# The gates' 16 columns ride behind the first head's values as moving columns

## The reference

```python
(sb, scg, sx, mq, mk, mv, mo, mg, dq, dk, dv, gs, gm, gd) = split_cols(u @ w_in + b_in)
...
g = mg.astype(jnp.float32).reshape(b, t, 4, ML_HEADS).transpose(2, 0, 3, 1)
gates = (g[0], g[1], jax.nn.log_sigmoid(g[2]), jax.nn.log_sigmoid(g[3]))
```

## Time and profile before

| | us |
|---|---|
| median of 3 runs | 2347.71 |
| lowest, highest | 2346.6, 2347.77 |
| span of the profiled execution | 2345.9 |
| TensorE busy in it | 2324.3 (99%) |
| VectorE busy | 1658.6 (71%) |
| ScalarE busy | 1034.5 (44%) |
| the 24 products of the gates, each layer | 5.44 |

### The profile page before, as it was taken

How to read it: one execution, slowest core, us unless ns; L and a number is a source line. 1 busy time by engine, 2 the same in 40 slices (tenths; PEclk the granted TensorE clock), 3 DMA queues, 4 the chain that set the end, 5 groups by cost and what they waited for, 6 DMA issues and landing times.

```text
span 2345.9 us, 35713 instructions
## 1 busy us (share of the span) xinstructions
PE 2324.3 (99%) x12926; PEld 2024.5 (86%) x12926; DVE 1658.6 (71%) x2777; ACT 1034.5 (44%) x1765; POOL 194.4 (8%) x186
## 2 busy tenths in 40 slices
PE   8999999999999999999999999999999999999998
PEld 6888889888888888898888898888898898999997
DVE  6998577457757655669885368886665757878876
ACT  5423224435556544363222264322245347756554
POOL 2111000000000000021120000111100000001220
PEclk9999999999999999999999999999999999999999
DMA  8788465232222322338783328776544433656654
GB/s 276 241 249 246 127 213 149 82 95 76 73 68 81 95 81 70 110 91 254 237 246 113 94 80 249 232 237 181 180 117 117 117 99 103 172 143 196 193 160 141
DMA packets 540057, 356.89 MB, mean 152 GB/s; under 512 B 15206, under 2 KB 490896, under 8 KB 539920
## 3 DMA queue, kind: packets, MB, share of 16 engines
q1 hardware_dynamic: 538472, 354.70, 51.6%
q10 hardware_dynamic: 1448, 0.38, 0.1%
HBM read 337.20 MB, written 17.83 MB: 151 GB/s over the span
## 4 chain that ended last, share of the span: by engine, by line
PE 94%; DVE 2%; ACT 1%; issue 1%; DMA 1%; POOL 0%; DVEq 0%; SPq 0%; ACTq 0%; POOLq 0%
PE ps L1101 25%; PE ps L1103 25%; PE ps L1102 25%; PE ps L1401 2%; PE ps L1402 2%; PE ps L1400 2%; PE ps L1114 1%; PE ps L1475 1%; PE ps L1193 1%; PE ps L1195 1%; PE ps L1194 1%; PE ps L1512 1%; PE ps L1116 1%; DVE w_lo L2350 0%; PE ps L1413 0%
## 5 line engine op out<-in xcount | busy, mean ns | idle before, releaser
L1618 ACT ACTIVATE w_hi<-raw 128x1024 fp32r<-128x1024 f32 (+3 forms) x430 | 423.3, 985 | 848.9 <-PE ps L1103 661.1
L2350 DVE TENSOR_TENSOR w_lo<-raw,w_hi 128x1024 fp32r<-128x1024 f32 (+3 forms) x430 | 495.0, 1152 | 423.1 <-ACT w_hi L1618 417.6
L1101 PE MATMUL ps<-u_hi,w_hi 128*128 128x512 f32 (+2 forms) x2176 | 778.1, 358 | 1.1 <-DVE w_lo L2350 0.7
L1103 PE MATMUL ps<-u_hi,w_lo 128*128 128x512 f32 (+2 forms) x2176 | 773.5, 355 | 0.0
L1102 PE MATMUL ps<-u_lo,w_hi 128*128 128x512 f32 (+2 forms) x2176 | 773.1, 355 | 0.0
L1101 PEld LDWEIGHTS ps<-u_hi,w_hi 128*128 128x128 f32 x2176 | 411.2, 189 | 60.1 <-issue 1.3
L1103 PEld LDWEIGHTS ps<-u_hi,w_lo 128*128 128x128 f32 x2176 | 411.1, 189 | 57.7
L1102 PEld LDWEIGHTS ps<-u_lo,w_hi 128*128 128x128 f32 x2176 | 411.4, 189 | 55.8
L2768 DVE SCALAR_TENSOR_TENSOR ada_acc<-ada_in_up,cs,ada_acc 128x512 f32<-128x512 f32 x378 | 284.2, 813 | 0.0
L1101 PE MATMUL ps<-g,w_hi 128*128 128x512 f32 (+1 forms) x572 | 206.9, 362 | 0.0
L1102 PE MATMUL ps<-g,w_hi 128*128 128x512 f32 (+1 forms) x572 | 204.1, 357 | 0.0
(11 more groups left out here) (394 smaller groups left out, 3678.0 us busy)
## 6 DMA issues: line engine op xcount, KB each, us to landing
raw<-in_ffn_up SPq DMA_DIRECT2D x150, 512.0 KB, 4.8
raw<-in_w_in SPq DMA_DIRECT2D x132, 512.0 KB, 3.8
ada_in_up<-in_w_ada SPq DMA_DIRECT2D x108, 512.0 KB, 4.6
raw<-in_ffn_down SPq DMA_DIRECT2D x67, 384.0 KB, 3.6
fold_out<-ada_acc SPq DMA_DIRECT2D x32, 512.0 KB, 3.5
fold<-fold_out SPq DMA_DIRECT2D x32, 512.0 KB, 5.4
raw<-in_ffn_down SPq DMA_DIRECT2D x42, 320.0 KB, 3.2
h<-in_ffn_up SPq DMA_DIRECT2D x22, 512.0 KB, 4.0
```

The source lines that it names most:

```text
L1101: pe.matmul(ps[bank][:, cols_of], wh, a_hi, start=a, stop=False)
L1103: m = pe.matmul(ps[bank][:, cols_of], wl, a_hi, start=False, stop=b)
L1618: act.activation(hi, whole, ACT.Copy).then_inc(hi_done, 1)
L2350: dve.tensor_tensor(lo, whole, hi.bitcast(F32), ALU.subtract).then_inc(lo_done, 1)
```

## The change

The gates' columns become moving columns. The first group of values is cut in two: chunks mv0 to mv3 hold head 0's 256 columns and behind them the gates' 16 (272 in all), mv4 to mv7 head 1's 256, mv8 to mv11 the last two heads' 512. Each of the first four has a second transfer for the 16 columns. The first values group now comes before mk0 to mk3, so the order is cg1, mv0 to mv3, mk0 to mk3, mv4 to mv11, sx1, sb1. On emptying the first group VectorE also copies the 16 columns of each token tile into a cleared tile `gate_rows`, spread in four groups, and TensorE turns that tile in four transposes behind mk0. The 24 products, the early transfer and `gate_weights` go. The gate steps stand behind mk0, mk3, mv5 and mv8.

```diff
-CH_UP, CH_DOWN, CH_PROJ, CH_WO = 2 * KF, 4 * KD, 48, KD
+CH_UP, CH_DOWN, CH_PROJ, CH_WO = 2 * KF, 4 * KD, 52, KD
...
-GATES_BEHIND = (0, 4, 5, 8)
+GATES_BEHIND = (4, 7, 9, 12)
...
-    for n in range(12):
-        order.append(("mk", n) if n < 4 else ("mv", n - 4))
-        if n in (6, 8):
-            order.append(("qk_high" if n == 6 else "qk_low", 0))
+    for n in range(16):
+        order.append(("mk", n - 4) if 4 <= n < 8 else ("mv", n if n < 4 else n - 4))
+        if n in (10, 12):
+            order.append(("qk_high" if n == 10 else "qk_low", 0))
...
+VALUE_TILES = (("mv", 0, 2), ("mv", 2, 2), ("mv", 4, 4), ("dv", 0, 4))
+GATE_COLS = 16
+VALUE_WIDTH = [n * P + (GATE_COLS if group == 0 else 0) for group, (_, _, n) in enumerate(VALUE_TILES)]
...
-                sp.dma_start(wg_in[:, :, :], w_in[layer, :, MG_COL:MG_COL + 16].rearrange("(k p) n -> p k n", p=P)
-                             ).then_inc(wg_landed, 16)
...
+                    sp.dma_start(dst[:, :, 0:n * P], src[:, k:k + 2, col:col + n * P]).then_inc(raw_in[slot], 16)
+                    if group == 0:
+                        sp.dma_start(dst[:, :, n * P:n * P + GATE_COLS], src[:, k:k + 2, MG_COL:MG_COL + GATE_COLS]
+                                     ).then_inc(gates_landed[step[1] % RAW], 16)
...
-                    pe.matmul(ps[t][:, :], u_hi[:, k, own], wh, start=(k == 0), stop=False)
-                    pe.matmul(ps[t][:, :], u_lo[:, k, own], wh, start=False, stop=False)
-                    m = pe.matmul(ps[t][:, :], u_hi[:, k, own], wl, start=False, stop=(k == KD - 1))
+                    pe.matmul(ps[t][:, 0:width], u_hi[:, k, own], wh, start=(k == 0), stop=False)
+                    pe.matmul(ps[t][:, 0:width], u_lo[:, k, own], wh, start=False, stop=False)
+                    m = pe.matmul(ps[t][:, 0:width], u_hi[:, k, own], wl, start=False, stop=(k == KD - 1))
...
-            pe.wait_ge(wg_ready, layer + 1)
-            for k in range(KD):
-                pe.wait_ge(u_ready, u_count(3 * layer + 1, 1, k))
-                for n, (w, a) in enumerate(((wg_hi, u_hi), (wg_hi, u_lo), (wg_lo, u_hi))):
-                    m = pe.matmul(ps[6][:, :], w[:, k, :], a[:, k, :], start=(n == 0 and k == 0),
-                                  stop=(n == 2 and k == KD - 1))
+            pe.wait_ge(evac_dve, BASES[layer, "proj"][2] + PLANS[layer]["mv", 3][3] + 1)
+            for t in range(TT):
+                m = pe.transpose(ps[6][:, t * P:(t + 1) * P], gate_rows[:, t, :], ident)
...
-            for w in (wg_hi, wg_lo):
-                pool.memset(w[:, :, :].bitcast(F32), 0.0).then_inc(wg_cleared, 1)
+            pool.memset(gate_rows[:, :, :], 0.0).then_inc(rows_cleared, 1)
...
-                if f == 0:
-                    gate_weights(layer)
...
+                if group == 0:
+                    m = dve.tensor_copy(gate_rows[:, t, :].rearrange("p (q n) -> p q n", q=4)[:, :, 0:HEADS],
+                                        ps[t][:, tiles * P:tiles * P + GATE_COLS].rearrange("p (q n) -> p q n", q=4))
+                m.then_inc(evac_dve, 1)
```

More of the change, by code:

```diff
@@ L325, with value_width @@
 BESIDE_ML = range(FIRST_ML - 3, FIRST_ML + 5 * HEADS)
-assert [NTH_PROJ[n] for n in (FIRST_ML - 5, FIRST_ML - 4)] == [("mv", 6), ("mv", 7)] and FIRST_ML % 4 == 3
+assert [NTH_PROJ[n] for n in (FIRST_ML - 5, FIRST_ML - 4)] == [("mv", 10), ("mv", 11)] and FIRST_ML % 4 == 3
 FIRST_AFTER = (0, 1, 3, 5)
-X_FIRST = ORDERS[0][4:ORDERS[0].index(("mk", 0))]
+X_FIRST = ORDERS[0][4:ORDERS[0].index(("mv", 0))]
 PROJ_BANK = [n % (2 if n in BESIDE_ML else 4) for n in range(CH_PROJ)]
 assert all(n % 4 == v[1] % 4 for n, v in NTH_PROJ.items() if v[0] in VALUES)
+assert all(PLANS[layer][step][0] == n for layer in range(DEPTH) for n, step in NTH_PROJ.items())
+def value_width(c):
+    step = NTH_PROJ.get(c)
+    if step is None or step[0] not in VALUES or VALUE_WIDTH[VALUES[step[0]] + step[1] // 4] == BLOCK:
+        return None
+    return VALUE_WIDTH[VALUES[step[0]] + step[1] // 4]
 SCORE_ML = (6, 7, 2, 3)
@@ L560, in apart_rows, with split_views @@
         return slice(3 * q - 3, 3 * q - 3 + len(LAST_K[q]) // 2), seg_order(n)[1][1]
-    def split_views(r, slot, raw_slot, kn):
+    def split_views(r, slot, raw_slot, kn, width=None):
         raw_view = raw_tiles(raw_slot, kn)
+        if width is not None:
+            return [a.rearrange("p (k n) -> p k n", k=2)[:, :, 0:width]
+                    for a in (w_hi[:, slot, :], w_lo[:, slot, :], raw[:, raw_slot, :])]
         if not is_apart(r):
@@ L1387, in values @@
             base, part = BASES[layer, "proj"][0], i % 4
-            slot = (base + r) % SPLIT
+            slot, width = (base + r) % SPLIT, VALUE_WIDTH[VALUES[kind] + i // 4]
             pe.wait_ge(lo_done, base + r + 1)
@@ L1610, in silu_table, with split @@
             act.activation(small[:, 15:16], small[:, 0:1], ACT.Silu)
-        def split(r, slot, place, kn=KD):
+        def split(r, slot, place, kn=KD, width=None):
             wait(act, chunk_used, split_room(r))
@@ L1616, in split, with ahead @@
             act.wait_ge(raw_in[raw_slot], landed)
-            hi, _, whole = split_views(r, slot, raw_slot, kn)
+            hi, _, whole = split_views(r, slot, raw_slot, kn, width)
             act.activation(hi, whole, ACT.Copy).then_inc(hi_done, 1)
-        def ahead(base, c, i=0, step=0, kn=KD):
+        def ahead(base, c, i=0, step=0, kn=KD, width=None):
             r = base + c + SPLIT
@@ L1624, in ahead @@
                 return
-            split(r + step * i, r % SPLIT, raw_place(base, c + SPLIT, i, step), kn)
+            split(r + step * i, r % SPLIT, raw_place(base, c + SPLIT, i, step), kn, width)
         for a, tile, r0, n in VECTOR_ROWS[0::2]:
@@ L1884, in proj @@
             t0 = t0_of(layer, kind in X_ONLY)
-            ahead(base, r)
+            later = NTH_PROJ.get(r + SPLIT, (None, 0))
+            if later[0] == "mv" and later[1] < 4:
+                act.wait_ge(gates_landed[later[1] % RAW], 16 * (2 * layer + later[1] // RAW + 1))
+            ahead(base, r, width=value_width(r + SPLIT))
             if kind in ("sx", "mk", "mv", "dv"):
@@ L2343, in after, with split, ahead @@
             dve.wait_ge(dve_chain, value)
-        def split(r, slot, place, kn=KD):
+        def split(r, slot, place, kn=KD, width=None):
             dve.wait_ge(hi_done, r + 1)
             wait(dve, chunk_used, split_room(r))
-            hi, lo, whole = split_views(r, slot, place[0], kn)
+            hi, lo, whole = split_views(r, slot, place[0], kn, width)
             dve.tensor_tensor(lo, whole, hi.bitcast(F32), ALU.subtract).then_inc(lo_done, 1)
-        def ahead(base, c, i=0, step=0, kn=KD):
+        def ahead(base, c, i=0, step=0, kn=KD, width=None):
             r = base + c + SPLIT
```

58 lines of the change are left out of this document (27 added, 31 removed).

## The result

The changed kernel takes 2363.57 us (median; 2362.27 to 2364.29) against 2347.0 us for the kernel before, run beside it: ratio 1.0069, 95% interval [1.0058, 1.0081]. It is 16.6 us slower. The forecast was 2358.5 us in a range that ended at 2363, 10.8 us above the 2347.7 that it started from; the direction held, the size was 5 to 6 us short. The difference of 0.69% lies well above the 0.2% that can be told here.

What follows compares the result with a forecast made beforehand. TensorE, busy for 99% of the span, was taken to bound the kernel. From 2347.7 us, layer 0 at +2.6 and layer 1 at +6.3 gave 2356.6; one clock fall, +2, made the forecast 2358.5 us, range 2355.5 to 2362.

Steps and rivals of the forecast that it cites:

- The arithmetic: TensorE's products and transposes, if nothing waits: -3.02 us per layer, -6.0 in all.
- The waits ahead of mv8: TensorE waits for VectorE to empty mv4's bank behind gate steps and splits: 5.4 us in layer 0, 4.5 in layer 1.
- mv0 in layer 1: First values chunk of layer 1 needs all four banks within 3 us and waits for their emptying: cost 3.6 us.
- mk0: mk0 waits for mv0's bank, emptied behind mk2's split: 0.1 us in layer 0, 1.1 in layer 1.
- What was costed at nothing: Extra loads, gate-column transfers, smaller splits, removed instructions and the gates' last step: covered, with no wait of their own.
- The clock: TensorE's clock falls behind one of the two long waits, about 2 us: +2, bounds 0 and 4.
- two falls: Rival: the clock falls behind both long waits, 2360.5 us; 75% together with the forecast and the no-fall case.
- worse: Rival: the gate columns' tiny rows hold up loads by over 1 us each, more short chunks starve: 2363 and up, 7%.
- One place alone: Rival: only layer 1's early queue costs, 2346.4 us, or only the waits before mv8, 2351.6 or 2353.6; 12%.
- the faster side: Rival: VectorE empties mv4's bank in time and mv0's banks are free: 2341.4 us, 6%.

Runs made afterwards that it cites:

- keys_first: Changed kernel with mk0 to mk3 ahead of mv0 to mv3 again and every gate step three or four chunks later: 2347.55 us.
- keys_split_only: keys_first with only the rounding and splitting of head 0's queries and keys moved forward, to behind chunks 8 and 9: 2347.9 us.
- steps_behind_narrow: Changed kernel with only gate steps 1 and 2 moved, step 1 two chunks forward, step 2 two chunks back behind the emptying: 2349.88 us.
- no_gate_transfer: Changed kernel without the eight transfers of the 16 gate columns and the wait for them, so gates use stale columns: 2360.69 us.
- warm_products: Changed kernel with 18 unused products of 512 columns written ahead of mv8's wait in each layer: 2358.86 us.
- keys_first_early_step3: keys_first with gate step 3 two chunks forward and head 0's queries and keys rounded and split behind chunks 8 and 9: 2343.95 us.
- wide_group_second: Changed kernel with the 512-column values group before the second 256-column group, gate steps behind mk0, mk1, mk3 and mv5: 2349.36 us.
- keys_step3_only: keys_first with only gate step 3 moved two chunks forward: 2346.12 us.

## Why the prediction was right or wrong

**The arithmetic**, -3.02 us a layer: -2.78 in layer 0 of keys_first and -2.76 in that of keys_split_only, where nothing waits. Right, 0.25 too good. In keys_first the four chunks of 272 columns take 12.26 us where I took 12.16, the four of 256 columns 11.71 for 11.52, and the 512-column group 21.86 for 21.76; the transposes give 0.14 of this back (0.36 for 0.5).

**The waits ahead of mv8**, 5.4 and 4.5: 5.15 and 4.33, by the chain that was written down. steps_behind_narrow shows the cause by its own removal, for the two gate steps together.

**mv0 in layer 1**, 3.6: 1.58 + 1.56, each with about 0.15 more from start to start than the row says, 3.4 in all. The last piece, for cg1's bank, is 0.4 where the clock stays up and was hidden under the fall where it did not. Right.

**mk0**, 0.1 and 1.1: 0.46 in layer 0, somewhat more than foretold; in layer 1 nothing in the changed kernel and 0.93 once the clock stays up. Right as a place; the fall stood in front of it.

**What was costed at nothing**: without the small transfers the long waits are the same (no_gate_transfer), and from one mixer to the next the time is unchanged. What was costed at nothing and wasn't is the clock at mv0: the prediction let it fall only behind the two long waits.

**The clock** is the step that failed: "Waits of 5.4 and 4.5 us may each set it off (bounds 0 and 4 us); I take one: +2." Both set it off, and a third fall came inside mv0. By spacing the first cost 2.9 us and the second, with ten slow intervals, 2.35; warm_products gave back 2.9 and 2.3 by undoing them. The third cost some 0.8. Together about 6.0 us where I took 2 and allowed 4. The size of one fall, 2 us, came from 16 transposes at the start of the trace: those took 3.6 us in all, while the slow stretches here last 6.1 us (504.27 to 510.38) and 4.8 (1840.04 to 1844.87). The sixteen were not the whole of that slow stretch either. The timeline of the kernel before goes on, behind four smaller products, with

```profile
13.98 2.85 PE L1032 MATMUL ps<-con,x_in 128*128 128x128 f32 x16
```

Read one by one, the first nine of these still start 0.213 us apart, up to 15.91, and the rest 0.109. So the slow stretch at the start lasted 6.1 us (9.84 to 15.91), and at the later spacing its products would have taken about half of that: an estimated 3 us lost, not 2. (That it is the low level is read from the spacing; the record of the granted clock begins at 15.9.) And the end of the trace had the clock down some 3 us after the last product; both waits were longer, and I had no row that spoke for one fall rather than two.

The sum by layer: 0 is -2.8 + 5.15 + 0.46 + 2.9 + 0.3 for two waits' extra = 6.0, measured 6.15. Layer 1 is -2.8 + 3.4 + 4.33 + 0.15 + 2.35 + 2.6 (the third fall at its face: 84 products from 1788.31 to 1801.46 are 13.15 us where 84 x 0.1258 are 10.57; the waits for cg1's and mk0's bank lie inside it) = 10.0, measured 10.09. The forecast's sum without a clock, 8.9, stands against 10.2 (16.2 less 6.0) measured: 1.3 of the miss is waits and arithmetic, 4.0 is the clock. The term that failed is therefore the clock's, in the number of falls (three for one) and in the size of one (2.9 and 2.3 for 2).

Of the rivals, "two falls" (2360.5) was the nearest in what happened. The time itself lies where "worse" had it (2363 and up), by luck: that rival had loads held up by the 16 columns, and without their transfers the long waits are the same. One place alone and the faster side did not happen. The faster side's condition held once I made it true: with the steps behind the emptying and keys first, the time is 2343.95, against 2341.4 given for that case.

What stays open: why the clock stayed down 5.5 us behind one wait and 2.6 behind an equal one, and the 2.15 us between the mixers of keys_first_early_step3, of which 1.5 us are waits for u_lo (nothing was tried on it).

## What to carry to other kernels

A chunk made half as long halves the time that another engine has for what is written beside it: before narrowing one, count what the in-order engine that frees its buffer has to do ahead of that, and move long work that nobody awaits (here the gates' scans) behind it. Price a gap of TensorE like those that brought a fall here as the gap and what slow products cost behind it: 2.9 and 2.3 us in the changed kernel, 1.5 in each layer of no_gate_transfer, and less where another wait follows within them and takes them up. And after a wait is taken away, look for the next: the 5 us gained here went into the wait for sx1's bank until step 3 and head 0's splitting were moved as well.

## What the runs showed of the hardware

The granted clock was 0.50 behind waits of 4.3 and 5.2 us. It fell also at one of 3.6 us (keys_first) and at the second of two of 1.6 us with 0.8 us of products between them, or up to 1.2 us behind it (steps_behind_narrow, at 1781.12), while a single wait of 1.51 us (keys_step3_only, layer 0) and one of 1.03 us (warm_products) left the spacing at 0.23 to 0.34 us. At the low level products of 512 columns start 0.426 us apart against 0.2267, of 272 columns 0.225 against 0.126, and of 256 columns 0.213 against 0.12. Full spacing came back 2.9 us (wide_group_second, 1780.44 to 1783.38) to 6.4 us (504.27 to 510.65) after the first product behind the wait. A wait costs about 0.15 us more from start to start than its row says.

Some 8 us of work that nothing reads, put into TensorE's idle time, made the kernel 4.7 us faster (2363.57 to 2358.86).
